# A score matmul issued ahead of the turn that waits, in the forgetting attention of a two-block kernel

## The reference

```python
log_f = log_sigmoid(f_logit + f_bias)
c = cumsum(log_f, axis=time)
for each head, each block of queries:
    s = q @ k.T / sqrt(64) + (c[query] - c[key])
    s = where(key <= query, s, -inf)
    o = softmax(s) @ v
```

## Time and profile before

| | us |
|---|---|
| median of 3 runs | 4401.55 |
| lowest, highest | 4398.78, 4418.33 |
| the profiled execution | 4401.55 |
| its span in the profile | 4399.9 |
| mean granted clock of TensorE | 0.902 of full |

### The profile page before, as it was taken

The page is one execution under the profiler, slowest core; times in us unless marked ns, Lnnn a source line. Parts: engine busy times, 40 slices in busy tenths (PEclk is TensorE's granted clock), DMA queues, the critical chain, the costliest instruction groups (busy, mean ns, idle before and its releaser), DMA issues. The chain is left out here.

```text
span 4399.9 us, 53944 instructions
## 1 busy us (share of the span) xinstructions
PE 3679.2 (84%) x21643; PEld 3160.2 (72%) x21643; DVE 1837.3 (42%) x2796; ACT 1152.1 (26%) x1993; POOL 287.6 (7%) x269
## 2 busy tenths in 40 slices
PE   7599969995769997788579997877877769999898
PEld 1499946664759995455578995556776559999776
DVE  1416535554441113354535203544554344555343
ACT  0313235554221113111224212432221121111232
POOL 0000000000100000110101100002121000000010
PEclk9699979997779995699679997988999879999999
DMA  6324350002203210121211211000000221111232
GB/s 233 133 91 159 117 191 11 11 11 78 77 30 104 76 61 16 64 72 49 82 62 35 63 59 46 20 9 1 1 0 1 82 63 48 48 43 47 90 121 86
DMA packets 199369, 284.74 MB, mean 65 GB/s; under 512 B 39510, under 2 KB 143766, under 8 KB 197158
## 3 DMA queue, kind: packets, MB, share of 16 engines
q1 hardware_dynamic: 180268, 222.02, 15.6%
q0 software_dynamic: 12704, 47.95, 3.4%
q10 hardware_dynamic: 6240, 12.58, 0.8%
HBM read 216.07 MB, written 66.44 MB: 64 GB/s over the span
## 5 line engine op out<-in xcount | busy, mean ns | idle before, releaser
L108 PE MATMUL p_pb<-p_w_hi,h_hi 128*128 128x416 f32 (+1 forms) x1280 | 444.4, 347 | 31.1 <-DVE p_w_lo L103 31.1
L110 PE MATMUL p_pb<-p_w_hi,h_lo 128*128 128x416 f32 (+1 forms) x1280 | 443.9, 347 | 0.0
L109 PE MATMUL p_pb<-p_w_lo,h_hi 128*128 128x416 f32 (+1 forms) x1280 | 442.6, 346 | 0.0
L108 PE MATMUL fu_pf<-h_hi,fu_w_hi 128*128 128x346 f32 (+2 forms) x1056 | 340.8, 323 | 18.3 <-DVE fu_pf L2934 18.3
L109 PE MATMUL fu_pf<-h_lo,fu_w_hi 128*128 128x346 f32 (+2 forms) x1056 | 341.9, 324 | 0.0
L110 PE MATMUL fu_pf<-h_hi,fu_w_lo 128*128 128x346 f32 (+2 forms) x1056 | 341.1, 323 | 0.0
L108 PEld LDWEIGHTS p_pb<-p_w_hi,h_hi 128*128 128x128 f32 x1280 | 241.7, 189 | 32.6 <-issue 31.9
L109 PEld LDWEIGHTS p_pb<-p_w_lo,h_hi 128*128 128x128 f32 x1280 | 241.7, 189 | 2.0
L110 PEld LDWEIGHTS p_pb<-p_w_hi,h_lo 128*128 128x128 f32 x1280 | 241.7, 189 | 0.8
L108 PEld LDWEIGHTS fu_pf<-h_hi,fu_w_hi 128*128 128x128 f32 x1056 | 199.4, 189 | 18.7 <-DVE fu_pf L2934 18.7
L110 PEld LDWEIGHTS fu_pf<-h_hi,fu_w_lo 128*128 128x128 f32 x1056 | 199.3, 189 | 0.0
(11 more groups left out here) (479 smaller groups left out, 7796.3 us busy)
## 6 DMA issues: line engine op xcount, KB each, us to landing
fu_raw<-in_ffn_up SPq DMA_DIRECT2D x88, 256.0 KB, 3.2
fd_raw<-in_ffn_down SPq DMA_DIRECT2D x44, 512.0 KB, 3.6
la_qkv<-p SPq DMA_DIRECT2D x16, 1024.0 KB, 5.0
p<-p_o SPq DMA_DIRECT2D x80, 194.0 KB, 1.9
p<-p_o SPq DMA_DIRECT2D x60, 208.0 KB, 1.9
p_raw<-in_gla_w_in POOLq DMA_DIRECT2D x16, 776.0 KB, 6.3
mod_w<-in_adaln_w SPq DMA_DIRECT2D x6, 2048.0 KB, 9.3
mod_w<-in_adaln_w ACTq DMA_DIRECT2D x6, 2048.0 KB, 8.9
```

Source lines behind the costliest of these rows:

```text
L108: pe.matmul(out, left[0], right[0], start=start, stop=False)
L109: pe.matmul(out, left[0], right[1], start=False, stop=False)
L110: return pe.matmul(out, left[1], right[0], start=False, stop=stop)
```

## The change

In every step, TensorE issues `score(u, 0)` ahead of the wait for `weights` and of `turn(u - 2, 0)`; before, it was issued behind them. `score(u, 1)`, if there is one, stays behind the turn. The one-time wait for the load of v (`v_in`, step 2) now stands behind a score too.

```diff
@@ -2333,13 +2333,14 @@
 
                 for u in range(NU + 2):
                     n = len(groups(u - 2)) if u >= 2 else 0
+                    if u < NU:
+                        score(u, 0)
                     if u == 2:
                         pe.wait_ge(v_in, 32)
                     if n:
                         pe.wait_ge(weights, u - 1)
                         turn(u - 2, 0)
                     if u < NU:
-                        score(u, 0)
                         score(u, 1)
                     if n > 1:
                         turn(u - 2, 1)
```

## The result

The changed kernel takes 4431.52 us (median of 20 runs, 4401.85 to 4455.17) against 4399.86 for the kernel before (20 runs, 4390.61 to 4431.21): a ratio of 1.0064, 95% interval 1.0047 to 1.0082. It is slower by 0.6%, where 4404 was forecast and 4420 was the top of the range. The profiled execution took 4431.23 us, with a span of 4429.5.

The account below looks back on a forecast made before the run. TensorE was taken to bound the attention stage, with only its idle time to win. Gaps opened (6.7 us a pair) less gaps filled (5.2), adjusted for the first pair's low clock, gave +1.5 to +2.5 on 4401.55: 4404 us, range 4386 to 4420.

Parts of the forecast that it names:

- The bound of the stage: Forgetting attention, 288 us: TensorE has most to do, busy 243.1 us; only its idle time can be won.
- the gap at the border: Ahead of the first turn at a pair's border: the 2.51 us gap shrinks only to 2.27 us.
- the third rival: Attention stage: new gaps of 0.4 to 0.7 us bring the clock down inside every pair; 32 us, 4436 us; chance 0.06.
- the direct loss: Per pair of heads at full clock: 6.7 us of gaps opened less 5.2 filled, 1.5 us more.
- two large terms: Per pair: 5.2 us gained ahead of the turn (fx_E), 6.7 us lost behind it (fx_ET).
- the joint: TensorE idling of 0.17 us between a multiplication and the next load; expected merely to move, costing 12 us at most.
- the bounds: Whole kernel: 4400 us if copy latency partly goes, 4416 us if each moved score pays one more 0.17 us of idling.
- the case of the long gap: After the 2.51 us gap at a pair's border the clock is 0.53 for 7.20 us, costing up to 3.3 us.
- my own row: A low-clock stretch like the first pair's, 10.8 us, in each of three pairs: 32 us.
- the direct bound: Upper bound, whole kernel: 72 x 0.17 = 12 us of added idling around moved scores, 4416 us.

Follow-up runs that it names:

- the filled borders: Matmuls nobody reads put in the gap at each pair's border: in the changed kernel 4428.42 us, ratio 1.0046; in the kernel before 4396.93 us, ratio 0.9994.
- the two halves of the change: Score moved ahead for wide units only (over 512 keys): 4401.4 us, ratio 1.0008; for narrow units only: 4397.85 us, ratio 0.9997.
- the four steps: Kernel before with the score moved ahead in only four of a pair's 18 steps, those with the longest gaps: 4396.75 us, ratio 0.9992.
- the warm start: Kernel before, order unchanged, with unread matmuls at pair borders and during the waits for first q and k and first weights: 4393.75 us, ratio 0.9983.

## Why the prediction was wrong

**What held.** The bound of the stage, the loop and the place of every gap: 7.7 us behind fx_E (forecast 15 or less), 29.8 behind fx_ET (30 or more, so just short of it), the second turn at 1.29 us, the gap at the border at 2.37 (2.3), the lower clock behind it. That the change loses rather than gains at full clock held too, though 4404 put it within what a measurement can't tell from nothing. Of the other signs, a pair of 68 to 69 us and a stage within 5 us of its length did not come: the third pair takes 79.2 us at a clock of 0.82 and the stage 32 us more. The sign for the third rival, a stretch under 0.9 in the middle of a pair, did.

**A term mis-sized: the direct loss.** At a clock of 1.00 a pair takes 64.58 us in the order of before (the borders filled) and 67.01 in the changed order (the borders filled): +2.4 us, not +1.5. The sum's two large terms came out smaller: the waits for fx_ET grow by 5.8 us (forecast 6.7) and those for fx_E fall by 5.0 (5.2), and all in all the pair's time without a matmul rises by 0.2 us, not 1.5. One reason for the 5.8 is that a second cut of 16 keys covers 0.29 us and not 0.14. What makes the loss is the joint, which the sum put at nothing: TensorE's busy time in the pair rises from 57.01 to 59.22 us, 2.2 us or about 0.12 for each of 18 scores, as in the score of 512 keys that takes 0.96 where 0.86 was taken. It stood in the bounds, where I set it aside with the argument that the joint "merely moves"; it doesn't. For the stage, 4 x 2.4 makes about 9 to 10 us, not 2.5. That +1.5 lies near +2.4 is in part luck, since its terms were off in both directions.

**The step that failed: the clock.** It is the third rival, at 0.06, with 4436 us as its time. I held against it that the gaps of 1.35 and 0.9 us in the second pair of the kernel before leave the clock at 1.00, and took from that that short gaps are harmless. The runs showed: with the short gaps idle and every border filled, the clock falls in mid-pair, at 2927, and stays at the lower level about 47 us, and the stage is at 0.81 as without the fills; with the short gaps worked through, the clock of the stage goes from 0.81 to 0.92 and 26.8 us of the 32.4 come back, although the direct cost is still there. That the gaps of before leave the clock at 1.00 was a right reading; it just doesn't carry over to the same idling in other places. By these estimates 9 to 10 us of the stage's 32 are direct and about 23 the clock (58 us more at the lower level at 0.39). So the rival's 4436 is close to the measured 4431.52 by luck: it had 32 us for the clock and 2.5 for the direct cost. The Trainium skill (TensorE: Matmul & The Clock Gate, "A second HAM failure mode") describes such a case, a bf16 kernel that cycles through PSUM banks, whose clock goes down and up as the engine idles briefly between groups of matmuls. The run with the filled borders agrees: there the clock fell at 2927 behind waits of 0.69 us and less. I had cited the case of the long gap from that page and left this one out.

**The range.** I took its top from the direct bound and the spread of three runs. What a clock that falls in mid-pair costs, 32 us by my own row, lay outside.

**Open.** When a row of short gaps brings the clock down and when not: the third pair of the same kernel has the gaps and stays at 1.00. Why the same idling does it in the changed order and not in that of before: one difference is its place, since now most of it lies behind the first turn, between two groups of transposes or ahead of a multiplication, where it lay ahead of the first turn; no run here tests that. And why the two halves of the change cost nothing each while the whole costs 0.6%.

## What to carry to other kernels

Before you move work ahead of a wait, ask what it covered where it stood: here the score hid ScalarE's copy, and the gap of VectorE's wait was exchanged for the gap of the copy, at about equal length and in slightly more places. Where TensorE's granted clock is seen to fall anywhere near, don't take gaps that it survives as proof that it survives gaps in another place: price the new idling twice, once as time and once as the chance that the clock falls, and let the range reach that far. Filling unavoidable gaps with matmuls that nobody reads is a cheap test of whether a loss is clock or order, and the part of a split group that is put ahead of the wait should be the part that nothing behind the wait needs as cover.

## What the runs showed of the hardware

The stage behind this one runs the same code in all kernels, and in the 14 profiled executions it came in two lengths: 449.7 to 453.3 us with a mean granted clock of 0.91 or 0.92 in nine, and 463.5 to 468.3 us with 0.87 to 0.89 in five. A gain of 10 to 20 us in one stage was given back in the next, most or all of it, in the profiled executions of the kernels with the four steps, with the filled borders and with the warm start. So on this program a stage's gain read from a single profile isn't yet a gain of the whole, and only the many timed runs tell. What decides between the two lengths is not shown.
